# One-hot products of the gates in two passes of the rounded 32-bit type

## The chip, the cores and the metric

One core of a Trainium2 chip runs the program. The time is device microseconds of one execution. The kernel before took 3685.89 us, the median of 3 runs (3681.72 to 3691.2).

## The reference

Two transformer blocks run one after the other on 512 tokens of width 1024. The change lies in the expert layer (`peer`) of the first block. It has 16384 experts, 128 x 128 keys, and 8 heads that each choose 16 experts for a token:

```python
expert = k1 * PEER_N_KEYS + k2
g = jax.nn.softmax(top_s.astype(jnp.float32), axis=-1).astype(hb.dtype)
ue = expert_u[expert]
act = jax.nn.gelu(jnp.einsum('td,thkd->thk', hb, ue), approximate=False) * g
ve = expert_v[expert]
return jnp.einsum('thk,thkd->td', act, ve)
```

`k1` and `k2` are the two key numbers (0 to 127) of each of a token's 128 choices, and `g` is the choice's gate.

## The kernel before

**Two ways through the experts.** For 384 of the 512 tokens (token tiles 0, 1 and 2, called DENSE) the kernel computes the scores of all 16384 experts: 128 blocks b of 128 experts, each 24 products of 128 weights by 384 columns (`linear(("U", b), ...)`). The last 128 tokens (tile 3, SPARSE) take only their chosen rows, gathered by indirect DMAs from GpSimd (L718) and multiplied and summed on VectorE (L1957).

**Rounded type.** Products of weights use a rounded 32-bit type (fp32r): ScalarE copies a weight tile WR to its rounded high part WH (L1200), VectorE subtracts to get the low part WL (L1601), and TensorE makes three rounded products (high by high, high by low, low by high), all on L787. Other products, the one-hot ones among them, use the plain 32-bit type, which the profile records as two passes.

**The gates of the dense tokens.** The dense scores have to be multiplied by a gate for every (expert, token) pair, zero where the expert was not chosen. For one token this is a 128 x 128 matrix: the sum over its 128 choices of onehot(k2) times gate times onehot(k1). The kernel makes it as one product with the choices on the 128 partitions. The keys and gates of a token tile are first transposed (`keys_out`, three transposes on L992, after VectorE has finished the gates in `gates`, L1941), and VectorE copies them to KT (`keys_in`, L1975). Then, for four tokens at a time, 96 times in all:

- VectorE makes hotA, 1.0 where the column number equals k1 (`hots`, L1984, one instruction for four tokens).
- ScalarE multiplies hotA in place by the gate (`hot_weights`, L1375, four instructions).
- GpSimd makes hotB, 1.0 where the column number equals k2 (L734, four instructions with one operation each).
- TensorE multiplies them (`hot_gates`, L983, four products of 128 x 128 by 128 columns).
- ScalarE copies the bank out to Gs (`gates_out`), and SP's queue stores it to memory every fourth time.

**Order.** All of this is written out block by block in the loops over b on each engine. In block b, TensorE does the scores, then the transposes if b is GATE_AT + 1, then the one-hot products of group b - HOT_LAG (HOT_LAG is 2), then in some blocks a tile of the modulation (L865 and a small product on L787). GpSimd does in block b the four L734 of group b and then the gathers that are due, in one queue. VectorE does in block b the hotA of group b, the low half of the next weights, some steps of the choice of the next token tile (`choose`) and the row dot L1957. hotA and hotB have four buffers each (HOTS). TensorE waits for hot_a (counted by ScalarE) and hot_b (counted by GpSimd) before a group. The groups run in the blocks 22 to 53, 54 to 85 and 86 to 117 (HOT_AT).

Of the kernel before, what the change touches and what calls it, by code (L numbers as in the profile page):

```python
# [6 lines left out]
P = 128  # L7
# [416 lines left out]
def build(nc, plan, d, out):  # L424
# [9 lines left out]
    with ctx:  # L434
# [91 lines left out]
        def col(t, tt):  # L526
            return t[:, tt * P:(tt + 1) * P]
# [24 lines left out]
        Q2 = place("Q2", F0 + 8192, 2, T)  # L552
        Rw = place("Rw", F0 + 8192, 16, P)
        cand = place("cand", F0 + 10240, PH, NC)
        hotA, hotB = place("hotA", F0 + 12288, HOTS, 4, P), place("hotB", F0 + 14336, HOTS, 4, P)
        f1 = F0 + 16384
        top, topi, topf = (place(n_, f1 + 256 * i_, 16, PK)[:, :, :] for i_, n_ in enumerate(("top", "topi", "topf")))
        cv, ca, cb, kk1, kk2, gg, cpos, cpa = (
# [2 lines left out]
        top_of = {tt: (tab[:, 2048:2304], tab[:, 2304:2560]) for tt in EARLY[1:]}  # L561
        top_of = {tt: tuple(t_.rearrange("p (i k) -> p i k", k=PK) for t_ in pair) for tt, pair in top_of.items()}
        Re = {tt: place(f"Re{tt}", F0 + at, 8, P) for tt, at in zip(EARLY, (9216, 10240))}
        gsum, KT = place("gsum", f1 + 1792, 1, 16), place("KT", f1 + 1824, 2, 3, P)
        hT = place("hT", F0 + 18976, D)
        geU = place("geU", F0 + 20000, 2, TN)
        sub = tab[:, 0:2048].rearrange("p (s n) -> p s n", s=16)
# [137 lines left out]
        @block.gpsimd  # L705
        def _(pool):
            k = Counts(pool, plan)

            pool.wait_ge(sgu_loaded, 64)
            nc.gpsimd.affine_select(out=ws, in_=ws, pattern=[[0, 4], [1, P]], compare_op=ALU.is_ge,  # L710
                                           fill=0.0, base=0, channel_multiplier=-1).then_inc(ws_ready, k.inc(ws_ready))

            def gather(i):

                if i >= ROWS:
                    pool.wait_ge(row_used, i - ROWS + 1)
                table, pick = ("urows", i) if i < PICKS else ("vrows", i - PICKS)
                nc.gpsimd.indirect_dma_start(  # L718
                    rows[:, i % ROWS, :], None, d[table][:, :],
                    bass.IndirectOffsetOnAxis(ap=expert[:, pick:pick + 1].bitcast(u32), axis=0),  # L720
                ).then_inc(row_loaded[i % ROWS], 16)

            issued = 0
            for b in range(NK):
                if hot_in(b):
                    tt, q = hot_in(b)
                    n = tt * (P // 4) + q
                    if q == 0:
                        pool.wait_ge(dve_read, k.reading(dve_read, ("kt", tt)))
                    if n >= HOTS:  # L730
                        pool.wait_ge(filled, k.filling(filled, ("g", (n - HOTS) // 32, (n - HOTS) % 32)))
                    for t in range(4):
                        c = 4 * q + t
                        nc.gpsimd.tensor_scalar(hotB[:, n % HOTS, t, :], consts["iota128"][:, :],  # L734
                                                KT[:, tt % 2, 1, c:c + 1], None, ALU.is_equal)\
                            .then_inc(hot_b, k.inc(hot_b))
                if b >= GATE_AT[SPARSE]:
                    if issued == 0:
                        pool.wait_ge(xt_stored, 16)
                        pool.wait_ge(picked, 1)  # L740
                    while issued < dots_by(b) + ROWS:
                        gather(issued)
                        issued += 1
            while issued < 2 * PICKS:
                gather(issued)
                issued += 1
# [3 lines left out]
        def _(pe):  # L750
# [225 lines left out]
            def hot_gates(tt, q):  # L976
                n = tt * (P // 4) + q
                pe.wait_ge(hot_a, 4 * (n + 1))
                pe.wait_ge(hot_b, 4 * (n + 1))

                def calls(b):
                    for t in range(4):
                        yield nc.tensor.matmul(col(b, t), hotB[:, n % HOTS, t, :], hotA[:, n % HOTS, t, :],  # L983
                                               start=True, stop=True)
                fill(("g", tt, q), calls)

            def keys_out(tt):
                pe.wait_ge(kt_ready, k.next(kt_ready))

                def calls(b):  # L990
                    for n, src in enumerate((kk1, kk2, gg)):
                        yield nc.tensor.transpose(col(b, n), src.rearrange("p a b -> p (a b)"), consts["ident"][:, :])  # L992
                fill(("kt", tt), calls)

            for b in range(NK):
# [184 lines left out]
        def _(act):  # L1180
# [188 lines left out]
            def hot_weights(tt, q):  # L1369
                n = tt * (P // 4) + q  # L1370
                act.wait_ge(hot_keys, n + 1)
                for t in range(4):
                    c = 4 * q + t
                    hot = hotA[:, n % HOTS, t, :]
                    act.activation(hot, hot, ACT.Copy, scale=KT[:, tt % 2, 2, c:c + 1]).then_inc(hot_a, k.inc(hot_a))  # L1375

            def gates_out(tt, q):
                n = tt * (P // 4) + q
# [212 lines left out]
        def _(dve):  # L1591
# [342 lines left out]
            def gates(done):  # L1934
# [6 lines left out]
                v.tensor_tensor(gg, gg, gsum[:, 0, 8:16].unsqueeze(2).to_broadcast([P, PH, PK]), ALU.mult)\  # L1941
                    .then_inc(done, k.inc(done))

            def picks():

                dve.wait_ge(*k.own())
# [23 lines left out]
            def keys_in(tt):  # L1970
                if tt == 2:

                    dve.wait_ge(filled, k.filling(filled, ("g", 0, 31)))
                b = bank_of(("kt", tt))
                v.tensor_copy(KT[:, tt % 2, :, :].rearrange("p a b -> p (a b)"), b[:, 0:3 * P])\  # L1975
                    .then_inc(dve_read, k.inc(dve_read))

            def hots(tt, q):
# [10 lines left out]
            for b in range(NK):  # L1989
# [14 lines left out]
                for tt in DENSE:  # L2004
                    if b == GATE_AT[tt]:
                        for _ in following:
                            pass
                        gates(kt_ready)
                        following, steps = choose(tt + 1) if tt + 1 < SPARSE else iter(()), STEP
                for _ in range(steps):  # L2010
                    next(following, None)
# [438 lines left out]
```

## Time and profile before

| | |
|---|---|
| median of the runs | 3685.89 us |
| profiled execution, own time | 3694.17 us |
| its span in the trace | 3692.3 us |
| TensorE matmul busy | 3524.6 us (95%) |
| TensorE weight load busy | 3031.6 us (82%) |
| VectorE busy | 2061.6 us (56%) |
| ScalarE busy | 1487.7 us (40%) |
| GpSimd busy | 730.6 us (20%) |
| mean granted TensorE clock | 0.974 |

The shares are averages over the whole span; the one-hot products lie between 847 and 1377 us. PE is TensorE's matmuls and PEld its weight loads, DVE is VectorE, ACT ScalarE, POOL GpSimd. Matmuls overlap, so a record's duration is longer than the time from one record's start to the next.

### The profile page before, as it was taken

Reading aid. Unit: us, or ns where it says so; the run is one execution under the profiler, and the core shown is the slowest. Engines: PE = TensorE matmul, PEld = TensorE weight load, DVE = VectorE, ACT = ScalarE, POOL = GpSimd, SP = SyncE. Lnnn points to the kernel's source line nnn. Section 1 sums busy time; section 2 is a strip of 40 time slices with the busy share of each in tenths; the row PEclk is TensorE's granted clock in tenths of the full one; section 3 lists DMA queues with packets and bytes.
Section 4 is the critical chain, followed back from the end, with each engine's and each line's share of the span. In section 5 each row is a group of like instructions: output and inputs, shape, how many; then the busy total and the mean of one; then the engine's idle time right before and its main releaser. Section 6 shows DMA issues by size and latency. Waiting matters only on the chain.

```text
span 3692.3 us, 54725 instructions
## 1 busy us (share of the span) xinstructions
PE 3524.6 (95%) x21345; PEld 3031.6 (82%) x21345; DVE 2061.6 (56%) x4243; ACT 1487.7 (40%) x2664; POOL 730.6 (20%) x645
## 2 busy tenths in 40 slices
PE   7999999989999999999998999999999979999997
PEld 5787887879899999999996568868888756777886
DVE  3253344677887557888884563284333246547443
ACT  3233324336666663333334462263112345436222
POOL 0000000008999884443330000000000000000000
PEclk8999999999999999999998999999999979999998
DMA  6224323469888999999993011101121211221232
GB/s 227 97 81 148 103 97 123 158 217 303 272 294 284 324 310 358 376 360 365 373 364 111 29 35 58 63 7 58 58 66 62 91 57 46 75 69 36 95 99 91
DMA packets 219679, 594.50 MB, mean 161 GB/s; under 512 B 17824, under 2 KB 101408, under 8 KB 216096
## 3 DMA queue, kind: packets, MB, share of 16 engines
q1 hardware_dynamic: 159312, 405.84, 31.8%
q0 software_dynamic: 36864, 134.23, 10.2%
q10 hardware_dynamic: 23248, 50.92, 3.7%
q8 instruction: 172, 2.82, 0.3%
q14 instruction: 83, 0.68, 0.1%
HBM read 530.11 MB, written 60.82 MB: 160 GB/s over the span
## 4 chain that ended last, share of the span: by engine, by line
PE 88%; DVE 5%; ACT 3%; DMA 2%; issue 2%; ACTq 0%; POOL 0%; DVEq 0%; SPq 0%
PE bank L787 64%; PE bank L1016 14%; PE bank L1108 3%; PE bank L983 2%; PE bank L1094 2%; PE bank L811 1%; PE bank L865 1%; DMA WR<-in_weights 1%; DMA rows<-in_urows,rk 1%; PE bank L898 0%; DVE WL L1601 0%; PE bank L970 0%; DVE OF L2297 0%; DVE SrowA L2151 0%; DVE X L2300 0%
## 5 line engine op out<-in xcount | busy, mean ns | idle before, releaser
L1601 DVE TENSOR_TENSOR WL<-WR,WH 128x1024 fp32r<-128x1024 f32 x512 | 631.4, 1235 | 838.5 <-ACT WH L1200 787.5
L1200 ACT ACTIVATE WH<-WR 128x1024 fp32r<-128x1024 f32 x512 | 536.7, 1057 | 739.3 <-PE bank L1016 303.7
L787 PE MATMUL bank<-H2h,WH 128*128 128x512 f32 (+1 forms) x1624 | 580.4, 357 | 4.5 <-DVE H2l L1629 4.5
L787 PE MATMUL bank<-H2h,WL 128*128 128x512 f32 (+1 forms) x1624 | 575.7, 354 | 0.0
L787 PE MATMUL bank<-H2l,WH 128*128 128x512 f32 (+1 forms) x1624 | 575.3, 354 | 0.0
L787 PE MATMUL bank<-Hh,WH 128*128 128x384 f32 (+1 forms) x1440 | 522.1, 363 | 13.8 <-DVE WL L1601 13.8
L787 PE MATMUL bank<-Hh,WL 128*128 128x384 f32 (+1 forms) x1440 | 508.3, 353 | 0.0
L787 PE MATMUL bank<-Hl,WH 128*128 128x384 f32 (+1 forms) x1440 | 507.8, 353 | 0.0
L734 POOL TENSOR_SCALAR hotB<-iota,KT 128x128 f32<-128x128 f32 x384 | 396.9, 1045 | 3.2
L1016 PE MATMUL bank<-ah,WH 128*128 128x384 f32 x1024 | 345.3, 337 | 6.5 <-issue 3.6
L787 PEld LDWEIGHTS bank<-H2h,WH 128*128 128x128 f32 x1624 | 309.1, 190 | 49.9 <-issue 7.7
L787 PEld LDWEIGHTS bank<-H2h,WL 128*128 128x128 f32 x1624 | 309.2, 190 | 43.7 <-issue 1.9
L1016 PE MATMUL bank<-ah,WL 128*128 128x384 f32 x1024 | 344.7, 337 | 0.0
L1016 PE MATMUL bank<-al,WH 128*128 128x384 f32 x1024 | 344.7, 337 | 0.0
L787 PEld LDWEIGHTS bank<-H2l,WH 128*128 128x128 f32 x1624 | 308.5, 190 | 42.7
L718 POOL DMA_INDIRECT rows<-in_urows,rk x128 | 149.0, 1164 | 856.7 <-DVE rk L1951 698.7
L787 PEld LDWEIGHTS bank<-Hh,WH 128*128 128x128 f32 x1440 | 274.0, 190 | 31.7 <-DVE WL L1601 14.3
L787 PEld LDWEIGHTS bank<-Hl,WH 128*128 128x128 f32 x1440 | 272.9, 189 | 16.6
L787 PEld LDWEIGHTS bank<-Hh,WL 128*128 128x128 f32 x1440 | 273.8, 190 | 14.8
L718 POOL DMA_INDIRECT rows<-in_vrows,rk x128 | 183.8, 1436 | 283.5 <-DVE acc L1968 260.7
L1016 PEld LDWEIGHTS bank<-ah,WH 128*128 128x128 f32 x1024 | 194.1, 190 | 7.7 <-issue 4.5
L1016 PEld LDWEIGHTS bank<-ah,WL 128*128 128x128 f32 x1024 | 194.2, 190 | 0.0
(349 smaller groups left out, 5562.0 us busy)
## 6 DMA issues: line engine op xcount, KB each, us to landing
WR<-in_weights SPq DMA_DIRECT2D x498, 512.0 KB, 3.8
WR<-in_vrows SPq DMA_DIRECT2D x128, 512.0 KB, 6.6
gelu_by_expert<-geU ACTq DMA_DIRECT2D x128, 192.0 KB, 5.1
gates_by_expert<-tab SPq DMA_DIRECT2D x24, 1024.0 KB, 9.5
geV<-gelu_by_expert SPq DMA_DIRECT2D x32, 768.0 KB, 9.2
Gt<-gates_by_expert SPq DMA_DIRECT2D x14, 1536.0 KB, 12.8
x_kept<-X ACTq DMA_DIRECT2D x2, 3072.0 KB, 8.6
X<-x_kept ACTq DMA_DIRECT2D x2, 3072.0 KB, 10.4
```

The costliest lines, as they stand in the source:

```text
L718: nc.gpsimd.indirect_dma_start(rows[:, i % ROWS, :], None, d[table][:, :], bass.IndirectOffsetOnAxis(ap=expert[:, pick:pick + 1].bitcast(u ...
L734: nc.gpsimd.tensor_scalar(hotB[:, n % HOTS, t, :], consts["iota128"][:, :], KT[:, tt % 2, 1, c:c + 1], None, ALU.is_equal)\
L787: yield nc.tensor.matmul(b[0:rows, out_cols], a, r, start=n == 0, stop=n == len(pairs) - 1)
L811: last = nc.tensor.matmul(b, a, r, start=j == 0 and n == 0, stop=j == KD - 1 and n == 2)
L865: yield nc.tensor.matmul(b[p0:p0 + QUAD, 0:P], cs[:, j, :], w[:, j, :], start=j < QUADS, stop=j >= KD - QUADS)
L983: yield nc.tensor.matmul(col(b, t), hotB[:, n % HOTS, t, :], hotA[:, n % HOTS, t, :], start=True, stop=True)
L1016: mm = nc.tensor.matmul(bank[sums[dd].bank][:, 0:TN], a, r, start=c == 0 and n == 0, stop=c == NK - 1 and n == 2)
L1094: yield nc.tensor.transpose(col(b, t - t0), col(Srow[kind][u % 4], t), consts["ident"][:, :])
L1108: yield nc.tensor.matmul(b[p0:p0 + VB, 0:P], v_[:, t, 0:VB], PT[kind][:, u % 2, n_, :], start=n_ < 2, stop=n_ >= len(tiles) - 2)
L1200: act.activation(WH[:, n % SLOTS, :, :].rearrange("p a b -> p (a b)"), WR[:, c % SLOTS, :, :].rearrange("p a b -> p (a b)"), ACT.Copy)\
L1601: v.tensor_tensor(WL[:, n % SLOTS, :, :].rearrange("p a b -> p (a b)"), WR[:, plan.splits[n] % SLOTS, :, :].rearrange("p a b -> p (a b)"), ...
```

## The change

The gate is split on VectorE into a high part, `ghi` (the gate rounded to fp32r), and `grest`, the remainder divided by the high part. Both are transposed (four transposes instead of three). GpSimd's hotB becomes onehot(k2) times the high part, by a second operation with a second per-partition scalar. hotA stays a plain one-hot and is kept; ScalarE writes hotA times the ratio into a new buffer, hotR. TensorE makes two products per token into the same bank, hotB by hotA and hotB by hotR, all in fp32r. KT moves to another place and gets a fourth column block.

```diff
--- before.py
+++ after.py
@@ -552,7 +552,8 @@
         Q2 = place("Q2", F0 + 8192, 2, T)
         Rw = place("Rw", F0 + 8192, 16, P)
         cand = place("cand", F0 + 10240, PH, NC)
-        hotA, hotB = place("hotA", F0 + 12288, HOTS, 4, P), place("hotB", F0 + 14336, HOTS, 4, P)
+        hotA, hotB, hotR = (place(n_, F0 + at, HOTS, 4, P, dt=f32r)
+                            for n_, at in (("hotA", 12288), ("hotB", 14336), ("hotR", 6144)))
         f1 = F0 + 16384
         top, topi, topf = (place(n_, f1 + 256 * i_, 16, PK)[:, :, :] for i_, n_ in enumerate(("top", "topi", "topf")))
         cv, ca, cb, kk1, kk2, gg, cpos, cpa = (
@@ -561,7 +562,8 @@
         top_of = {tt: (tab[:, 2048:2304], tab[:, 2304:2560]) for tt in EARLY[1:]}
         top_of = {tt: tuple(t_.rearrange("p (i k) -> p i k", k=PK) for t_ in pair) for tt, pair in top_of.items()}
         Re = {tt: place(f"Re{tt}", F0 + at, 8, P) for tt, at in zip(EARLY, (9216, 10240))}
-        gsum, KT = place("gsum", f1 + 1792, 1, 16), place("KT", f1 + 1824, 2, 3, P)
+        gsum, KT = place("gsum", f1 + 1792, 1, 16), place("KT", F0 + 11264, 2, 4, P)
+        ghi, grest, grec = place("ghi", f1 + 1824, P, dt=f32r), place("grest", f1 + 1952, P), place("grec", f1 + 2080, P)
         hT = place("hT", F0 + 18976, D)
         geU = place("geU", F0 + 20000, 2, TN)
         sub = tab[:, 0:2048].rearrange("p (s n) -> p s n", s=16)
@@ -732,7 +734,8 @@
                     for t in range(4):
                         c = 4 * q + t
                         nc.gpsimd.tensor_scalar(hotB[:, n % HOTS, t, :], consts["iota128"][:, :],
-                                                KT[:, tt % 2, 1, c:c + 1], None, ALU.is_equal)\
+                                                KT[:, tt % 2, 1, c:c + 1], KT[:, tt % 2, 2, c:c + 1],
+                                                ALU.is_equal, ALU.mult)\
                             .then_inc(hot_b, k.inc(hot_b))
                 if b >= GATE_AT[SPARSE]:
                     if issued == 0:
@@ -981,15 +984,18 @@
                 def calls(b):
                     for t in range(4):
                         yield nc.tensor.matmul(col(b, t), hotB[:, n % HOTS, t, :], hotA[:, n % HOTS, t, :],
-                                               start=True, stop=True)
+                                               start=True, stop=False)
+                        yield nc.tensor.matmul(col(b, t), hotB[:, n % HOTS, t, :], hotR[:, n % HOTS, t, :],
+                                               start=False, stop=True)
                 fill(("g", tt, q), calls)
 
             def keys_out(tt):
                 pe.wait_ge(kt_ready, k.next(kt_ready))
 
                 def calls(b):
-                    for n, src in enumerate((kk1, kk2, gg)):
-                        yield nc.tensor.transpose(col(b, n), src.rearrange("p a b -> p (a b)"), consts["ident"][:, :])
+                    keys = [kk.rearrange("p a b -> p (a b)") for kk in (kk1, kk2)]
+                    for n, src in enumerate((*keys, ghi[:, :].bitcast(f32), grest[:, :])):
+                        yield nc.tensor.transpose(col(b, n), src, consts["ident"][:, :])
                 fill(("kt", tt), calls)
 
             for b in range(NK):
@@ -1371,8 +1377,8 @@
                 act.wait_ge(hot_keys, n + 1)
                 for t in range(4):
                     c = 4 * q + t
-                    hot = hotA[:, n % HOTS, t, :]
-                    act.activation(hot, hot, ACT.Copy, scale=KT[:, tt % 2, 2, c:c + 1]).then_inc(hot_a, k.inc(hot_a))
+                    act.activation(hotR[:, n % HOTS, t, :], hotA[:, n % HOTS, t, :].bitcast(f32), ACT.Copy,
+                                   scale=KT[:, tt % 2, 3, c:c + 1]).then_inc(hot_a, k.inc(hot_a))
 
             def gates_out(tt, q):
                 n = tt * (P // 4) + q
@@ -1941,6 +1947,21 @@
                 v.tensor_tensor(gg, gg, gsum[:, 0, 8:16].unsqueeze(2).to_broadcast([P, PH, PK]), ALU.mult)\
                     .then_inc(done, k.inc(done))
 
+            def gate_parts():
+
+                flat = gg.rearrange("p h j -> p (h j)")
+                dve.wait_ge(*k.own())
+                v.tensor_copy(ghi[:, :], flat).then_inc(dve_step, k.inc(dve_step))
+                dve.wait_ge(*k.own())
+                v.tensor_scalar(grec[:, :], ghi[:, :].bitcast(f32), 1e-30, None, ALU.max)\
+                    .then_inc(dve_step, k.inc(dve_step))
+                v.tensor_tensor(grest[:, :], flat, ghi[:, :].bitcast(f32), ALU.subtract)\
+                    .then_inc(dve_step, k.inc(dve_step))
+                dve.wait_ge(*k.own())
+                v.reciprocal(grec[:, :], grec[:, :]).then_inc(dve_step, k.inc(dve_step))
+                dve.wait_ge(*k.own())
+                v.tensor_tensor(grest[:, :], grest[:, :], grec[:, :], ALU.mult).then_inc(kt_ready, k.inc(kt_ready))
+
             def picks():
 
                 dve.wait_ge(*k.own())
@@ -1972,7 +1993,7 @@
 
                     dve.wait_ge(filled, k.filling(filled, ("g", 0, 31)))
                 b = bank_of(("kt", tt))
-                v.tensor_copy(KT[:, tt % 2, :, :].rearrange("p a b -> p (a b)"), b[:, 0:3 * P])\
+                v.tensor_copy(KT[:, tt % 2, :, :].rearrange("p a b -> p (a b)"), b[:, :])\
                     .then_inc(dve_read, k.inc(dve_read))
 
             def hots(tt, q):
@@ -2005,7 +2026,8 @@
                     if b == GATE_AT[tt]:
                         for _ in following:
                             pass
-                        gates(kt_ready)
+                        gates(dve_step)
+                        gate_parts()
                         following, steps = choose(tt + 1) if tt + 1 < SPARSE else iter(()), STEP
                 for _ in range(steps):
                     next(following, None)
```

## Rows read from the trace of the kernel before

**Rows 1.** Busy time by stretch: start:end us, length, then busy us and count per engine.
```profile
900.00:1000.00 100.00, 92.74 (x626) 88.88 (x626) 82.05 (x179) 60.40 (x123) 96.77 (x84) 0.98 0.79 265
1000.00:1100.00 100.00, 100.00 (x683) 98.69 (x682) 78.15 (x218) 68.42 (x139) 96.61 (x97) 1.00 0.93 313
```

**Rows 2.** Chain of waits from 865 to 900 us: start us, us, what.
```profile
870.39 0.89 PE bank L983 x8
871.28 4.16 PE bank L787 x24
...
881.38 0.57 PE bank L865 x16
881.96 4.58 PE bank L787 x26
```

**Rows 3.** Groups by line from 846 to 1378 us, busy us, mean ns, idle before.
```profile
L734 POOL TENSOR_SCALAR hotB<-iota,KT 128x128 f32<-128x128 f32 x377 | 392.0, 1051 | 3.2
...
L983 PE MATMUL bank<-hotA,hotB 128*128 128x128 f32 x768 | 103.7, 279 | 14.1 <-ACT hotA L1375 7.8 <-issue 6.3
```

**Rows 4.** GpSimd's line L734 alone: duration ns min/median/max, first and last start.
```profile
L734 POOL TENSOR_SCALAR hotB<-iota,KT x384: 590/627/3452, 838.1 to 1371.6; 128x128 f32<-128x128 f32 x192
```

**Rows 5.** GpSimd in order of time, 892 to 903 us: start us, us, what.
```profile
892.23 4.61 POOL L734 TENSOR_SCALAR hotB<-iota,KT 128x128 f32<-128x128 f32 x4
897.01 1.03 POOL L718 DMA_INDIRECT rows<-in_urows,rk  x1 [0.17 <-issue]
898.07 4.54 POOL L734 TENSOR_SCALAR hotB<-iota,KT 128x128 f32<-128x128 f32 x4
```

**Rows 6.** TensorE in order of time, same stretch, its one-hot products.
```profile
896.94 1.13 PE L983 MATMUL bank<-hotA,hotB 128*128 128x128 f32 x8 [0.29 <-issue]
...
902.71 1.13 PE L983 MATMUL bank<-hotA,hotB 128*128 128x128 f32 x8 [0.46 <-issue]
```

**Rows 7.** GpSimd in order of time, 1040 to 1050 us.
```profile
1040.04 3.85 POOL L734 TENSOR_SCALAR hotB<-iota,KT 128x128 f32<-128x128 f32 x4
1044.05 1.03 POOL L718 DMA_INDIRECT rows<-in_urows,rk  x1 [0.16 <-issue]
1045.11 4.31 POOL L734 TENSOR_SCALAR hotB<-iota,KT 128x128 f32<-128x128 f32 x4
```

**Rows 8.** VectorE in order of time, 1041.5 to 1043.6 us.
```profile
1041.63 1.26 DVE L1957 SCALAR_TENSOR_TENSOR rows<-rows,hT 128x1024 f32<-128x1024 f32 x1
...
1042.82 0.68 DVE L1984 TENSOR_TENSOR hotA<-iota,KT 128x512 f32<-128x512 f32 x1
```

**Rows 9.** TensorE in order of time: first and last of 19 rounded products, 256 columns.
```profile
189.75 0.28 PE L787 MATMUL bank<-WH,Hl 128*128 128x256 f32 x1
...
191.91 0.28 PE L787 MATMUL bank<-WH,Hl 128*128 128x256 f32 x1
```

**Rows 10.** TensorE's weight loads in order of time, from 848.5 us.
```profile
848.58 0.30 PEld L787 LDWEIGHTS bank<-fold,mrow 128*128 128x128 f32 x2 [0.20 <-issue]
848.80 0.19 PEld L787 LDWEIGHTS bank<-Hh,WH 128*128 128x128 f32 x1
```

**Rows 11.** Weight loads of the whole span by line and shape.
```profile
L787 PEld LDWEIGHTS bank<-Hh,WH 128*128 128x128 f32 x1440 | 274.0, 190 | 31.7 <-DVE WL L1601 14.3 <-issue 2.3
...
L983 PEld LDWEIGHTS bank<-hotA,hotB 128*128 128x128 f32 x768 | 99.4, 194 | 17.6 <-ACT hotA L1375 9.0 <-issue 8.6
L1108 PEld LDWEIGHTS bank<-PTB,vB 128*64 128x64 f32 x832 | 43.8, 136 | 13.8 <-issue 13.1 <-ACT PTB L1226 0.6
```

**Rows 12.** GpSimd's groups by line, the smallest.
```profile
L2441 POOL MEMSET const-float32-1.0<- 128x1 f32 x1 | 0.1, 99 | 0.0
```

**Rows 13.** VectorE's groups by line and shape.
```profile
L1647 DVE RECIPROCAL rt<-rt 128x128 f32<-128x128 f32 x5 | 4.7, 942 | 25.8 <-ACT rt L1226 25.8
...
L1736 DVE TENSOR_SCALAR SV<-SV,mv,rs 128x1024 f32<-128x1024 f32 x4 | 3.0, 812 | 0.1
...
L1965 DVE TENSOR_SCALAR acc<-rows,rk 128x1024 f32<-128x1024 f32 x2 | 1.5, 746 | 0.0
...
L1947 DVE COPY rk<-gg 128x128 f32<-128x128 f32 x1 | 0.2, 228 | 0.0
```

**Rows 14.** In order of time: VectorE's last step of the gates, TensorE's first transposes.
```profile
825.75 0.29 DVE L1941 TENSOR_TENSOR gg<-gg,gsum 128x128 f32<-128x128 f32 x1
...
831.22 0.38 PE L992 MATMUL bank<-ident,kk 128*128 128x128 f32 x2
```

## The prediction

> **What bounds the kernel now.** I read the busy time by stretch first. In [rows 1] the stretch from 900 to 1300 us is the one with the one-hot products, and two engines are full there at once. TensorE is busy 92.7 of 100 us in the first window and 100.0 of 100 in the second, and GpSimd 96.8 and 96.6. VectorE is at 82 and 78, ScalarE at 60 and 68. The chain of waits gives TensorE's rhythm [rows 2]: a block is 4.16 us of expert scores (24 products of 384 columns, 0.173 us each) and 0.89 us of one-hot products (4 products recorded as 8 passes, 0.111 us a pass). Every fourth block adds 0.57 us (L865) and some 0.42 us (two passes on L787) of modulation. So a block is 5.05 us, or 6.05 us with modulation, 5.30 us on average, and there are 96 with one-hot products.
>
> Grouping the stretch by line [rows 3] shows the change's share: L983 is 768 passes, which at 0.111 us of pitch are 85 us of TensorE; L734 on GpSimd is 377 instructions with a mean of 1051 ns, though the line's own view [rows 4] gives a shortest of 590 and a median of 627. Something stretches them, so I looked at GpSimd in order of time. At 892 to 903 us [rows 5] four L734 take 4.61 and 4.54 us, with 1.03 us of a gather between them, and start 5.84 us apart. The first group ends at 892.23 + 4.61 = 896.84, the next at 902.61. TensorE's one-hot products start at 896.94 and 902.71, each 0.10 us later, after 0.29 and 0.46 us idle [rows 6]. The profile calls that idle "issue", but the two ends fit a wait for hotB. So GpSimd already sets the pace in places. Where it does not, it is close behind: at 1040 us a group takes 3.85 us and the next starts 5.07 us after it [rows 7], TensorE's own 5.05. Why the instruction stretches is in VectorE's order of time: its two-input operations on the row dot (1.26 us) and on hotA (0.68 us) run from 1041.63 to 1043.50 [rows 8], and GpSimd's group ends at 1043.89, just after them.
>
> **TensorE's part.** Four products of the 32-bit type (8 passes) become eight of the rounded type, one pass each. The trace has no rounded product under 256 columns, so I bound one. Low end: 256 columns start 0.120 us apart ((191.91 - 189.75)/18, [rows 9]) and 384 columns 0.173 [rows 2]; on that line 128 columns are 0.067 us, a group 0.53 us, 0.36 us less than 0.89. High end: each is carried as dearly as a 32-bit product (2 x 0.111 = 0.223), a group 1.78 us, 0.89 more. Middle: the weight load sets the pitch. Two loads of 128 weights before products of only 3 columns start at 848.58 and the next product's load at 848.80, 0.11 us each with nothing else to wait for [rows 10]. Load durations are 136 ns for 64 weights and 190 ns for 128 [rows 11], 0.84 ns a weight, so 128 of them stream for about 0.11 us. The rounded product's load (on WH) lasts 190 ns, like the 32-bit one's 194. With 384 columns that load hides behind 0.173 us of columns; with 128 it cannot. So I take 0.111 to 0.120 us each, a group of 0.89 to 0.96 us: 0 to +0.07 us, over 96 groups 0 to +7 us.
>
> The Trainium skill states the load as columns over 1.2 GHz, which is 107 ns for 128 (TensorE: Matmul & The Clock Gate, LDWEIGHTS); the loads in [rows 10] agree with it. The Trainium skill's same page gives about 81 ns for load and product at 128 columns (Back-to-back issue gap). By that a group would be an estimated 0.65 us and TensorE would shed 23 us; no row here shows such a pitch.
>
> **GpSimd's part.** Each of the 384 L734 gets a second operation (a product) with a second per-partition scalar, and a rounded output. Low end: no dearer, 0 (the first operation and its columns stay, so a gain is excluded). High end: the shortest L734 lasts 590 ns [rows 4], and an instruction with almost nothing to do (a memset of one column) 99 ns [rows 12]; if the second operation costs all that the first does beyond that, it adds 0.49 us. The nearest rows are VectorE's: over 1024 columns one operation with one scalar is 746 ns, two with two scalars 812 ns [rows 13], 66 ns more. GpSimd is the slower engine per column (0.49 us over 128 columns, against 0.75 us over VectorE's 1024), so I lean upward from that row and take twice its difference, 0.12 us.
>
> A group grows by 4 x 0.12 = 0.48 us. What covers it? In [rows 7] nothing but the 0.16 us gaps: GpSimd is already busy 96.6 of 100 us, and its cycle is as long as TensorE's. When GpSimd falls behind, TensorE waits for hotB, and ScalarE's and VectorE's work of the next block starts from TensorE's; so VectorE's interference repeats once a block and does not shrink. Hence +0.48 us on each of 96 blocks, 46 us, and TensorE's 0 to 7 us disappear inside that wait. The lead that GpSimd has at the start (a few us) is spent once; I subtract 4.
>
> **VectorE's and ScalarE's part.** The hotA comparison and the scaling on L1375 keep their sizes; the scaling writes hotR where it wrote hotA, and ScalarE has 32 to 40 us of every 100 free [rows 1]. Three times, VectorE gets five small operations. Four at about the 0.23 us of the 128-column copy (L1947), and a reciprocal of 128 columns, 0.94 us [rows 13]: 1.9 us with gaps. The transposes wait for them: the gates were ready at 825.75 + 0.29 = 826.04 and the transposes started at 831.22 [rows 14], so 5.2 us of cover remain 3.3 us. Behind them on VectorE is the low half of the next weights (L1601), one block ahead of its use; at the third place VectorE is near full, so I count 2 us of the 3 x 1.9. The fourth transpose costs 3 x 0.11 and the wider copy as little: 0.5 us.
>
> **The sum.** 46 - 4 + 2 + 0.5 = 44, rounded up to 47 for the clock that falls a little where TensorE waits more (0.98 in the window at 900 with 7.3 us idle, [rows 1]). The profiled execution took 3694.2 us (span 3692.3 and 1.9 around it), 8.3 above the median of the runs, 3685.9. So 3741 for that one, 3733 as a median.
>
> **The rivals.**
> (1) The rounded product of 128 columns is as dear as a 32-bit one. For: no row shows one under 256 columns. Against: the line from 384 to 256 columns shows no bend. A block grows 0.89 us, GpSimd's added 0.48 hides behind it, and the waits for hotB that exist today (up to the 14.1 us idle before L983, [rows 3]) go: 96 x 0.89 = 85, less 10, 3761.
> (2) The other side: the weight load does not set the pitch and the second operation is free on GpSimd. Then TensorE's block is 4.69 us and GpSimd's cycle decides how much is kept. GpSimd ran at 5.07 us between starts in [rows 7] and 5.84 in [rows 5], and the DMA engines are busy 0.93 of the window at 1000 us [rows 1]; of 0.36 x 96 = 34 us I let 20 through: 3666. It decides only if the addition on GpSimd is under about 0.05 us an instruction. The Trainium skill speaks for this half: a GpSimd body of at most two operations is bound by its port, not by its operations (GPSIMD Engine Reference, Elementwise). No row here has two operations there.
> (3) Both are neutral: the pitch is 0.111 and GpSimd's addition is under 0.03 us. 3690.
> (4) GpSimd's second operation is near its upper bound (0.3 us or more): 96 x 1.2 = 115, 3800.
>
> **How the numbers follow.** The forecast has 0.42, rival (1) 0.22, (2) 0.13, (3) 0.14, (4) 0.09. What a measurement can tell from no change is 0.3%, 11 us. Faster: 0.12, from (2). Slower: the forecast, (1) and (4), 0.73, less its small tail, 0.71. The rest, 0.17, is within. The range runs from 3672 to 3795: it leaves out the deeper half of (2) and most of (4).
>
> **What would show it.** L983's pitch: eight records in 0.89 us to 0.96 (forecast), 0.53 (rival 2), 1.78 (rival 1). L734's shortest duration: about 0.1 us longer. TensorE idle before L983 in most blocks, ending 0.10 us after a GpSimd group, and VectorE emptier by share. Wrong would be a TensorE that is full through the stretch with blocks of 5.05 us, or L734 unchanged.

## The result, and the profile after

The changed kernel took 3757.12 us (median of 4 runs, 3755.31 to 3759.35), the kernel before on the same chip 3683.80 us (4 runs, 3681.35 to 3691.20). The ratio is 1.0196, with an interval of 1.0181 to 1.0210: 72 us slower, where the forecast had added 47. The forecast was 3733, and the measured time lies inside the range of 3672 to 3795. The profiled execution after took 3755.31 us, its span 3753.4 and the mean granted clock 0.971.

The stage with the one-hot products holds the difference. Before, its first and last product (L983) started at 847.0 and 1376.1 us, 529.1 us apart; after, those of L986 and L988 at 846.6 and 1442.2, 595.6 us apart, 66.5 more. The first fence is the busy time by stretch of the kernel before, for that stage and for a later window than [rows 1] shows; the second is the kernel after, with the stage and the windows that answer to [rows 1]. Columns: start:end, length, then busy us and count of TensorE, its weight loads, VectorE, ScalarE and GpSimd, then the granted clock, the DMA share and GB/s.

```profile
846.90:1376.10 529.20, 513.61 (x3490) 502.32 (x3489) 385.77 (x824) 342.83 (x697) 493.98 (x467) 0.99 0.89 298
1200.00:1300.00 100.00, 97.08 (x652) 95.49 (x651) 55.79 (x75) 62.72 (x131) 88.42 (x86) 0.98 0.94 327
```

```profile
846.60:1442.20 595.60, 541.79 (x3489) 522.78 (x3490) 388.78 (x834) 346.70 (x698) 574.25 (x468) 0.95 0.79 264
900.00:1000.00 100.00, 88.12 (x569) 84.27 (x568) 72.34 (x180) 55.32 (x114) 96.90 (x79) 0.96 0.79 261
1000.00:1100.00 100.00, 92.57 (x594) 89.52 (x594) 73.02 (x177) 59.86 (x119) 95.59 (x80) 0.94 0.75 248
1200.00:1300.00 100.00, 89.35 (x588) 86.18 (x587) 59.99 (x79) 58.60 (x116) 96.86 (x81) 0.97 0.81 288
```

Read the stage rows as two balances. On GpSimd, busy time grew by 80.3 us (493.98 to 574.25) with the same instructions, and its idle time fell from 35.2 to 21.4, by 13.9: together the 66.4 us. On TensorE, with the same number of matmuls, idle time grew from 15.6 to 53.8 us and busy time from 513.61 to 541.79; the clock granted went from 0.99 to 0.95, so the same work took longer between the waits. In the windows shown GpSimd is now full (95.6 to 96.9 of 100 us) and TensorE is not (88 to 93), where [rows 1] had TensorE at 100.0 in one of them.

The profiled execution of the kernel before was 8 to 10 us above the medians of that kernel, and its stage was long. In run e4 (below), where all engines do the same work and only GpSimd's output type differs, the stage is this:

```profile
846.40:1365.10 518.70, 508.82 (x3489) 499.45 (x3489) 384.29 (x815) 342.60 (x697) 490.76 (x469) 1.00 0.90 304
```

Against it the stage after is 76.9 us longer, with 83.5 more of GpSimd's busy time and 6.6 less of its idle time. The 66.5 and the 76.9 us stand on either side of the 72 of the medians.

Next, the line of the hotB comparison alone, after (duration ns min/median/max, first and last start), answering to [rows 4], and the groups by line from 846 to 1450 us, answering to [rows 3] (busy us, mean ns, idle before).

```profile
L736 POOL TENSOR_SCALAR hotB<-iota,KT x384: 780/806/3458, 837.2 to 1438.9; 128x128 fp32r<-128x128 f32 x192
```

```profile
L736 POOL TENSOR_SCALAR hotB<-iota,KT 128x128 fp32r<-128x128 f32 x378 | 453.0, 1206 | 3.7
...
L720 POOL DMA_INDIRECT rows<-in_urows,rk x92 | 124.0, 1348 | 21.6 <-issue 14.6 <-DVE rows L1978 7.0
...
L986 PE MATMUL bank<-hotA,hotB 128*128 128x128 f32 x384 | 92.2, 277 | 54.2 <-issue 30.9 <-ACT hotR L1380 23.3
```

The shortest hotB comparison went from 590 to 780 ns, 0.190 us longer, the median from 627 to 806. The mean went from 1051 to 1206, 0.155 more: 384 x 0.155 = 60 us. The gathers on the same engine stood so before, in the groups by line from 846 to 1376 us:

```profile
L718 POOL DMA_INDIRECT rows<-in_urows,rk x90 | 103.1, 1146 | 30.6 <-DVE rows L1957 16.5 <-issue 14.1
```

They went from 1146 to 1348 ns, 0.202 more: 92 x 0.202 = 19 us. 60 + 19 = 79 of the 80.3 us. And what they waited for VectorE's row dot fell from 16.5 us to 7.0. TensorE's idle time before the one-hot products went from 14.1 to 54.2 us. Its list of waits in the same stretch says how often (who <- for whom: us, times, longest):

```profile
PE bank L986 <- issue: 30.9, 23, 4.2
PE bank L986 <- ACT hotR L1380: 23.3, 17, 2.6
```

These are 40 waits, in 96 blocks.

The rhythm behind it is in GpSimd's order of time, after, answering to [rows 5]; beneath it TensorE's first product of each block.

```profile
1057.31 5.39 POOL L736 TENSOR_SCALAR hotB<-iota,KT 128x128 fp32r<-128x128 f32 x4
1062.87 1.82 POOL L720 DMA_INDIRECT rows<-in_urows,rk  x1 [0.17 <-issue]
...
1071.06 4.21 POOL L736 TENSOR_SCALAR hotB<-iota,KT 128x128 fp32r<-128x128 f32 x4
1075.44 1.74 POOL L720 DMA_INDIRECT rows<-in_urows,rk  x1 [0.17 <-issue]
1077.22 4.05 POOL L736 TENSOR_SCALAR hotB<-iota,KT 128x128 fp32r<-128x128 f32 x4
```

```profile
1062.80 0.30 PE L986 MATMUL bank<-hotA,hotB 128*128 128x128 f32 x1 [1.22 <-ACT hotR L1380]
...
1075.37 0.30 PE L986 MATMUL bank<-hotA,hotB 128*128 128x128 f32 x1 [1.06 <-ACT hotR L1380]
...
1081.37 0.30 PE L986 MATMUL bank<-hotA,hotB 128*128 128x128 f32 x1 [0.70 <-issue]
```

The groups of four end at 1057.31 + 5.39 = 1062.70, 1071.06 + 4.21 = 1075.27 and 1077.22 + 4.05 = 1081.27. TensorE starts 0.10 us after each, after 1.22, 1.06 and 0.70 us idle. The releaser named is ScalarE's hotR twice and "issue" once; the ends fit GpSimd's group all three times.

Where GpSimd is ahead, TensorE's own block is what it was. This is the chain of waits after, around 1050 us, answering to [rows 2] (start us, us, what).

```profile
1047.22 4.22 PE bank L790 x24
1051.44 0.06 PE bank L986
1051.50 0.11 PE bank L988
...
1052.29 4.22 PE bank L790 x24
```

Eight rounded products start 0.11 us apart, and the block is 1052.29 - 1047.22 = 5.07 us where it was 5.05.

### The profile page after: what moved, and what is told of

Its sections match the earlier page's. It is cut to its first block, busy times and chain, and to the rows that moved or that the text cites. A ratio compares the mean times of both kernels' runs of the same rounds, so it can differ in the third digit from the quotient of the medians.

```text
span 3753.4 us, 54746 instructions
## 1 busy us (share of the span) xinstructions
PE 3547.4 (95%) x21348; PEld 3045.0 (81%) x21348; DVE 2065.4 (55%) x4258; ACT 1491.6 (40%) x2664; POOL 810.5 (22%) x645
## 4 chain that ended last, share of the span: by engine, by line
PE 87%; DVE 5%; ACT 3%; DMA 3%; issue 2%; POOL 0%; ACTq 0%; SPq 0%; DVEq 0%
PE bank L790 63%; PE bank L1022 13%; PE bank L1114 2%; PE bank L1100 2%; DMA WR<-in_weights 1%; PE bank L868 1%; PE bank L986 1%; PE bank L814 1%; PE bank L988 1%; DMA rows<-in_urows,rk 1%; DVE WL L1607 1%; ACT hotR L1380 1%; PE bank L901 0%; DVE SrowA L2173 0%; PE bank L973 0%
## 5 line engine op out<-in xcount | busy, mean ns | idle before, releaser
L790 PE MATMUL bank<-Hh,WL 128*128 128x384 f32 (+1 forms) x1440 | 516.3, 359 | 0.0
L790 PE MATMUL bank<-Hl,WH 128*128 128x384 f32 (+1 forms) x1440 | 515.8, 358 | 0.0
L736 POOL TENSOR_SCALAR hotB<-iota,KT 128x128 fp32r<-128x128 f32 x384 | 458.4, 1201 | 3.8
L720 POOL DMA_INDIRECT rows<-in_urows,rk x128 | 169.7, 1326 | 840.2 <-DVE rk L1972 697.0
```

The source lines that it names most:

```text
L720: nc.gpsimd.indirect_dma_start(rows[:, i % ROWS, :], None, d[table][:, :], bass.IndirectOffsetOnAxis(ap=expert[:, pick:pick + 1].bitcast(u ...
L790: yield nc.tensor.matmul(b[0:rows, out_cols], a, r, start=n == 0, stop=n == len(pairs) - 1)
```

## The experiments

Each ratio is to the kernel before on the same chip; "after with" and "before with" say which kernel was edited. e9b_wide_one_op and e10_half_weights are one run each, so their times carry no interval.

**One operation in hotB** (after with).
```diff
-    KT[:, tt % 2, 1, c:c + 1], KT[:, tt % 2, 2, c:c + 1], ALU.is_equal, ALU.mult)
+    KT[:, tt % 2, 1, c:c + 1], None, ALU.is_equal)
```


> The changed kernel with one thing undone: hotB is made by one operation again (the comparison alone, written in the rounded type); its factor, the gate's high part, is left out, so the gates are wrong and the work is otherwise the same. Theory G (GpSimd's second operation is the loss): the shortest hotB instruction falls from 780 ns to about 590, the idle time before TensorE's one-hot products from 54 us to about 14, and the time to 3680 to 3692 us (before 3684). Theory T (the eight rounded products, or the extra VectorE steps, are the loss): GpSimd is quicker but the time stays above 3735 us.

Measured: 3684.84 us, ratio 0.9989 (0.9978 to 1.0001). All of the loss is gone, with the eight rounded products, the gates' five steps and the fourth transpose still there. The first line is that of hotB alone in this kernel, the second is from its groups by line, 846 to 1378 us.
```profile
L736 POOL TENSOR_SCALAR hotB<-iota,KT x384: 590/627/3455, 840.2 to 1362.4; 128x128 fp32r<-128x128 f32 x192
```
```profile
L985 PE MATMUL bank<-hotA,hotB 128*128 128x128 f32 x384 | 86.2, 264 | 4.7 <-issue 3.5 <-ACT hotR L1379 1.1
```
The instruction is back at 590 ns, and TensorE waits 4.7 us before the products instead of 54.2.

**The second operation alone, in the kernel before**, with a second per-partition scalar (a column of ones), and then with a constant. The third puts only the rounded output type into the kernel before.
```diff
-    KT[:, tt % 2, 1, c:c + 1], None, ALU.is_equal)
+    KT[:, tt % 2, 1, c:c + 1], ones[:, 0:1], ALU.is_equal, ALU.mult)   # e2; e3 has 1.0 for ones[:, 0:1]
```


> The kernel before with one part of the change alone: the second operation on GpSimd, a product with a per-partition scalar (a column of ones, so the values stay). Theory G: shortest instruction 780 ns, time 3745 to 3765 us. Theory T: no more than 3700 us.

> As the run before it, but the second scalar is the constant 1.0 in the instruction. It splits the 190 ns: if fetching a second per-partition scalar costs it, the shortest instruction is near 590 to 640 ns and the time 3684 to 3705 us; if the second operation over 128 columns costs it, 780 ns and 3745 to 3765 us. I expect the larger part from the operation: 700 to 780 ns, about 3735 us.

```diff
-    hotB = place("hotB", F0 + 14336, HOTS, 4, P)
+    hotB = place("hotB", F0 + 14336, HOTS, 4, P, dt=f32r)
-    nc.tensor.matmul(col(b, t), hotB[:, n % HOTS, t, :], ...)
+    nc.tensor.matmul(col(b, t), hotB[:, n % HOTS, t, :].bitcast(f32), ...)
```


> The kernel before with hotB written in the rounded type by one operation and read as plain 32-bit by TensorE, so only GpSimd's output type changes. If rounding is part of the 190 ns, the shortest instruction is above 620 ns and the time above 3695 us; if not (what I expect), 590 ns and 3684 us, within 0.3%.

Measured: e2 3751.63 us, ratio 1.0174 (1.0155 to 1.0194); e3 3715.50, 1.0073 (1.0055 to 1.0092); e4 3685.71, 0.9996 (0.9985 to 1.0007). The line of hotB alone in the three kernels:
```profile
L734 POOL TENSOR_SCALAR hotB<-iota,KT,ones x384: 780/804/3422, 834.4 to 1430.9; 128x128 f32<-128x128 f32 x192
```
```profile
L734 POOL TENSOR_SCALAR hotB<-iota,KT x384: 704/730/3457, 837.0 to 1393.0; 128x128 f32<-128x128 f32 x192
```
```profile
L734 POOL TENSOR_SCALAR hotB<-iota,KT x384: 590/627/3451, 839.2 to 1360.6; 128x128 fp32r<-128x128 f32 x192
```
So the 0.190 us are 704 - 590 = 114 ns for the operation and 780 - 704 = 76 ns for taking its scalar from a tile; the rounding costs nothing. The one edit of e2, with every other part of the change absent, gives 65 of the 72 us, and the intervals of e2 and of the change overlap. The second operation with its second scalar is therefore the cause: it alone brings the loss (e2), and its removal alone takes it away (e1). The duration in e3 came as expected (700 to 780 ns), its time is a miss: I expected about 3735, and it came 20 us lower. Its windows (columns as above) show why:
```profile
1000.00:1100.00 100.00, 94.08 (x636) 89.81 (x635) 71.69 (x201) 63.94 (x127) 96.78 (x86) 0.98 0.79 265
1200.00:1300.00 100.00, 98.75 (x674) 97.13 (x673) 57.81 (x81) 66.00 (x136) 91.59 (x90) 1.00 0.96 340
```
In the first, GpSimd is full and TensorE is not; in the second, TensorE is at 98.75 and GpSimd at 91.59. In the later part of the stage GpSimd has spare time, 88.42 busy of 100 in the kernel before and 93.50 in the same window of e4, and much of an addition of 0.46 us a group still fits there. I had read [rows 1] as the whole stage.

**Half of the products** (after with).
```diff
-    yield matmul(col(b, t), hotB[...], hotA[...], start=True, stop=False)
-    yield matmul(col(b, t), hotB[...], hotR[...], start=False, stop=True)
+    yield matmul(col(b, t), hotB[...], hotA[...], start=True, stop=True)
```


> The changed kernel with the second product of each token left out (the low part of the gate is missing), so TensorE has 4 rounded products in a group and not 8: about 0.45 us less in each of 96 blocks, 43 us if TensorE set the pace. Theory G (GpSimd sets it): the freed time turns into waiting for hotB, at most 10 us are gained, the time is 3745 to 3757 us. Theory T: 3714 us.

Measured: 3768.37 us, ratio 1.0228 (1.0200 to 1.0255), a miss by time: I expected at most 3757, no slower than the changed kernel (1.0196). The two intervals overlap. From its groups by line, 846 to 1378 us, and its busy time by stretch:
```profile
L986 PE MATMUL bank<-hotA,hotB 128*128 128x128 f32 x336 | 54.7, 288 | 76.5 <-issue 44.4 <-ACT hotR L1378 31.8
```
```profile
1000.00:1100.00 100.00, 83.58 (x486) 80.23 (x487) 71.56 (x162) 54.91 (x108) 97.09 (x76) 0.88 0.71 229
```
TensorE was relieved of four products a block and only waited more: 76.5 us by 1378 us of the span, at a granted clock of 0.88 in that window. GpSimd stayed at 97. So TensorE's part of the change carries none of the loss. The 11 us between the two medians (on different chips) are not explained. In the profiled stages they sit in GpSimd's busy time (584.10 us in e5, 574.25 in the changed kernel), with the mean of hotB at 1249 ns against 1206; what stretches it more, no run separates.

**Two of the four hotB comparisons on VectorE** (after with, nothing left out).
```diff
-    for t in range(4):                       # GpSimd
+    for t in range(2):
-    pe.wait_ge(hot_b, 4 * (n + 1))
+    pe.wait_ge(hot_b, 2 * (n + 1))
+    pe.wait_ge(hot_d, 2 * (n + 1))
...
+    for t in range(2, 4):                    # VectorE, behind hotA
+        c = 4 * q + t
+        v.tensor_scalar(hotB[:, n % HOTS, t, :], iota128, KT[:, tt % 2, 1, c:c + 1],
+                        KT[:, tt % 2, 2, c:c + 1], ALU.is_equal, ALU.mult).then_inc(hot_d, k.inc(hot_d))
```


> The changed kernel, complete, with GpSimd's work halved: of the four hotB instructions of a group VectorE makes two (one instruction each with both operations, I estimate 0.25 us), GpSimd the other two. Theory G: GpSimd falls to about 70% busy, the idle time before the one-hot products nearly vanishes, and the time is at most that of the kernel before: 3672 to 3690 us. A rival: VectorE, at 72 to 78% in that stretch, cannot take 0.5 us more a block, and the weights' low halves come late: above 3700 us.

Measured: 3688.62 us, ratio 1.0011 (1.0001 to 1.0021). The whole change is kept, and 68 of 72 us are back. Its busy time by stretch, its VectorE hotB line, and TensorE's line:
```profile
1000.00:1100.00 100.00, 100.00 (x684) 98.88 (x683) 95.33 (x265) 66.20 (x138) 70.65 (x58) 1.00 0.91 301
```
```profile
L2012 DVE TENSOR_SCALAR hotB<-iota,KT x192: 331/390/953, 841.5 to 1358.9; 128x128 fp32r<-128x128 f32 x192
```
```profile
L988 PE MATMUL bank<-hotA,hotB 128*128 128x128 f32 x384 | 86.3, 264 | 2.0 <-ACT hotR L1382 2.0
```
TensorE is back at 100.00 of 100 and waits 2.0 us before the products. GpSimd has fallen to 70.65, and VectorE took its place as the fullest helper, 95.33. The rival that the weights' low halves come late is there in small: TensorE's list of waits, 846 to 1378 us, has this line:

```profile
PE bank L791 <- DVE WL L1609: 9.6, 2, 4.8
```

**The same in the kernel before** (edit as above, with `None, ALU.is_equal`).

> The kernel before, complete, with VectorE making two of the four hotB instructions of a group. Theory G says GpSimd was the co-limit already: the 14 us idle before the one-hot products go, 3672 to 3680 us. If those waits had another cause, or VectorE has no room: 3684 us or more.

Measured: 3684.35 us, ratio 0.9994 (0.9985 to 1.0003), a miss: I expected a gain. From its groups by line (846 to 1378 us), and from its list of waits in the same stretch (who <- for whom: us, times, longest):
```profile
L985 PE MATMUL bank<-hotA,hotB 128*128 128x128 f32 x768 | 101.3, 275 | 1.6 <-ACT hotA L1377 1.6
```
```profile
PE bank L788 <- DVE WL L1603: 7.6, 2, 3.8
```
The same two in e4, whose engines do the work of the kernel before, without the length of that one execution:
```profile
L983 PE MATMUL bank<-hotA,hotB 128*128 128x128 f32 x768 | 101.5, 275 | 6.9 <-issue 3.5 <-ACT hotA L1375 3.3
```
```profile
PE bank L787 <- DVE WL L1601: 3.0, 2, 1.5
```
So about half of the 14.1 us of waiting that I had expected back belonged to the profiled execution of the kernel before alone. From 6.9 to 1.6 us are 5.3 less, and the waits for the low half of a weight (WL) went from 3.0 to 7.6, 4.6 more: the busier VectorE hands it over late. The two cancel, as the times do. TensorE, full at 100.00 of 100 around 1000 us, has little left to win without less work of its own.

**What a single pass is worth** (before with one rounded product for each), alone and with the hotB split.
```diff
-    hotA, hotB = place("hotA", ...), place("hotB", ...)
+    hotA, hotB = place("hotA", ..., dt=f32r), place("hotB", ..., dt=f32r)
...
-    act.activation(hot, hot, ...)
+    act.activation(hot, hot.bitcast(f32), ...)
```


> The kernel before with its four products made rounded (one pass each, hotA with the gate rounded; the gate's low part is left out) and everything else as it was. TensorE has 0.45 us less in a block, 43 us over 96. If GpSimd was already the co-limit in the kernel before, as the prediction read it, most of that is lost to waits for hotB: a gain of 10 to 20 us, 3666 to 3676 us. If GpSimd had slack there: 3643 us.

> As the run before it (the gate's low part left out), and VectorE makes two of the four hotB instructions of a group. It takes away GpSimd's limit: 3640 to 3655 us if GpSimd was what held the run before back; the same as that run if it was not.

Measured: e11 3680.49 us, ratio 0.9987 (0.9974 to 1.0000), a miss: I expected a gain of 10 to 20 us. One of its ten runs took 13374.73 us, for a reason that nothing shows; the median of the other nine is 3678.79. e12 3650.37 us, ratio 0.9906 (0.9881 to 0.9931), as expected. TensorE's line, 846 to 1378 us, in e11 and in e12:
```profile
L983 PE MATMUL bank<-hotA,hotB 128*128 128x128 f32 x384 | 57.6, 273 | 35.1 <-ACT hotA L1375 19.7 <-issue 15.4
```
```profile
L985 PE MATMUL bank<-hotA,hotB 128*128 128x128 f32 x384 | 54.1, 263 | 3.7 <-ACT hotA L1377 3.6
```
Half of TensorE's one-hot passes gone is 96 x 4 x 0.111 = 43 us of its work. Alone that returns 5 to 7 us (3685.32 to 3680.49, or 3678.79) and turns into 35.1 us of waiting; relieving GpSimd alone returned 3 (e8, within noise); both together return 35 us. This shows that GpSimd was as much the bound as TensorE in the kernel before. e12 beats both kernels, by leaving out the gate's low part.

**What sets the pitch of a 128-column product** (after with one operation in hotB). The first makes one product over 256 columns (hotA and hotR together) in place of two, the second loads 64 weights in place of 128 with the columns unchanged.
```diff
-    yield matmul(col(b, t), hotB[...], hotA[...], start=True, stop=False)
-    yield matmul(col(b, t), hotB[...], hotR[...], start=False, stop=True)
+    yield matmul(b[:, (t % 2) * 256:(t % 2) * 256 + 256], hotB[...], hotAR[:, 0:4:3, at:at + P], start=True, stop=True)
```


> A measurement of TensorE's rounded product, in the changed kernel with hotB made by one operation: the two products of a token become one with 256 moving columns (hotR and hotA side by side), so one weight load of 128 serves both; tokens 2 and 3 overwrite the results of 0 and 1, and the sum of the two parts is left out. Theory L (the load of 128 weights sets the pitch of the 128-column product): four products start 0.120 us apart, 0.48 us a group where the changed kernel has 0.89. If instead a rounded product costs by its columns alone, the 256 columns take 0.21 us.

```diff
-    yield matmul(col(b, t), hotB[:, n % HOTS, t, :], hotA[...], ...)
+    yield matmul(col(b, t)[0:64], hotB[:, n % HOTS, t, 0:64], hotA[...], ...)   # hotR alike
```


> A measurement: the changed kernel with hotB made by one operation, and each of the eight products of a group with only 64 weights (the first half of hotB's columns; half of the result's rows are left out), 128 moving columns as before. Theory L: the pitch falls from 0.11 us to 0.06 to 0.07 us. Theory C (a rounded product of 128 columns runs at two cycles a column whatever the load): it stays at 0.11 us.

The chain of waits of the first kernel, then TensorE in order of time in the second:
```profile
1024.24 0.47 PE bank L986 x4
1024.71 4.17 PE bank L789 x24
```
```profile
1017.82 0.22 PE L985 MATMUL bank<-hotA,hotB 128*64 128x128 f32 x1
1017.88 0.22 PE L987 MATMUL bank<-hotR,hotB 128*64 128x128 f32 x1
...
1018.24 0.22 PE L987 MATMUL bank<-hotR,hotB 128*64 128x128 f32 x1
```
Twice the columns with one load: 0.47 / 4 = 0.12 us a product, hardly more than the 0.11 of 128 columns. Half the weights with the same columns: (1018.24 - 1017.82) / 7 = 0.060 us. The pitch halves with the weights and barely moves with the columns, so at 128 columns the weight load sets it. Both took about the time of the kernel before (3690.21 and 3680.03 us): TensorE's 40 us fewer bought nothing visible, much as in e11.

## Why the prediction was right, and where its sizes were off

**What bounds the kernel.** Right: GpSimd was full and as slow as TensorE. e11 and e12 show it directly, 5 to 7 us against 35 for the same relief of TensorE.

**TensorE's part, 0 to +7 us.** Right: the load sets the pitch (e10, e9b), the block went from 5.05 to 5.07 us, and with hotB back at one operation the kernel is at 0.9989 of before (e1). With [rows 10] the load's 0.11 us was there to be read before any 128-column rounded product existed. Rival (1) would have shown as a group of 1.78 us and falls; so does rival (2), which needed both a pitch of 0.067 and a free operation. One reason of the prediction was empty: two points, 256 and 384 columns, always lie on a line, so "no bend" said nothing about 128.

The Trainium skill gives 107 ns for the load of 128 weights (TensorE: Matmul & The Clock Gate, LDWEIGHTS), and the 0.11 us here agree. Its 81 ns for load and product at 128 columns (same page, Back-to-back issue gap) is not met by this type.

**GpSimd's part, +46 us.** The mechanism was right, the duration mis-sized: I took 0.12 us for the second operation, twice VectorE's 66 ns of [rows 13]; it measured 0.190 (780 against 590). By that the term is 4 x 0.190 x 96 = 73 us. The row that I doubled already held both prices, the operation and the second scalar from a tile (at 128 columns VectorE's two together are 61 ns, 270 against 331). What failed is the factor of two from VectorE to GpSimd, for which I had no row; it is about three (190 against 61). That the operation by a constant costs 0.114 us, close to my 0.12, is chance. Rival (4) had the right direction and too much of it; rival (3) needed under 0.03.

The Trainium skill's rule that a GpSimd body of at most two operations is bound by its port (GPSIMD Engine Reference, 3.1 Elementwise) is about the cost of each element, and would make the addition there nothing. e3 shows 114 ns for the operation alone at 128 columns, and the measurement decides for this instruction. Whether these 114 ns come with each element or once in each instruction is open, since no run varies the columns.

**"What covers it?"** My answer, nothing but the gaps of 0.16 us, failed in part. In the stage GpSimd gave up 13.9 us of idle time, 9.5 of them waits for the row dot before a gather (6.6 us against the stage of e4, so the size is known only roughly); in the window at 1200 us it had been busy only 88.42 of 100. I subtracted 4. e2 lost 65 us where 73 were added, e3 29 or so (3715.50 against 3686.19) where 44 were. Both errors, a price too low and a cover too small, pulled against each other. The step held in the part of the stage that [rows 1] shows, and I carried it to the rest.

**What I left out.** GpSimd's gathers became 0.202 us longer on average, 19 us in all; the hotB comparisons' stretch over their shortest shrank from 0.461 to 0.426 us (mean less minimum). That the interference "does not shrink" was thus nearly right for hotB and missed the gathers. e2 shows the same longer gathers without any other part of the change (mean 1382 ns up to 1376 us), so the new steps of VectorE do not make them. Nor does GpSimd's slower instruction: e11 has them too, with hotB at its 590 ns. Its lines from 846 to 1376 us:

```profile
L734 POOL TENSOR_SCALAR hotB<-iota,KT 128x128 fp32r<-128x128 f32 x380 | 370.0, 986 | 3.2
L718 POOL DMA_INDIRECT rows<-in_urows,rk x94 | 126.6, 1346 | 31.1 <-DVE rows L1957 16.5 <-issue 14.6
```

There the gathers took 23.5 us more than in the kernel before (103.1) and the comparisons 22.0 less (392.0), with a sum of 496.6 us against 495.1. What is common to e2, e11 and the changed kernel is a TensorE that waits for GpSimd; it looks as if the same interference falls on the gathers instead of the comparisons. So the 19 us of the gathers and the 13 by which the stretch of hotB shrank belong together, about 6 us net. The mechanism was not tried.

**VectorE's part, +2 us, and the fourth transpose, +0.5.** The five steps took 2.0 us, from 824.51 to 826.52, where I had 1.9. Here is VectorE after in order of time:
```profile
824.51 0.23 DVE L1954 CAST ghi<-gg 128x128 fp32r<-128x128 f32 x1
824.77 0.23 DVE L1956 TENSOR_SCALAR grec<-ghi 128x128 f32<-128x128 f32 x1
824.92 0.29 DVE L1958 TENSOR_TENSOR grest<-gg,ghi 128x128 f32<-128x128 f32 x1
825.24 0.95 DVE L1961 RECIPROCAL grec<-grec 128x128 f32<-128x128 f32 x1
826.23 0.29 DVE L1963 TENSOR_TENSOR grest<-grest,grec 128x128 f32<-128x128 f32 x1
```
The transposes started at 830.1 and waited for none of it: cover as forecast. Outside the stage the profiled spans leave 3163.2 us before and 3157.8 after, so nothing of these terms is to be seen there. Since e1 carries them all and is at 0.9989, they cost nothing that can be measured, where I had counted 2.5.

**The clock.** I rounded up 3 us for it. It fell more, from 0.99 to 0.95 over the stage, and TensorE's busy time grew by 28 us for the same matmuls. It was lowest in this window of the changed kernel:

```profile
1300.00:1400.00 100.00, 90.35 (x563) 87.50 (x562) 47.72 (x66) 55.81 (x114) 96.92 (x79) 0.91 0.78 259
```

GpSimd is as full there (96.92) as in the windows at a clock of 0.96 or 0.97. So I read TensorE's slower work as filling time in which it would have waited, and count nothing for it beside the 66 us of GpSimd's balance. No run holds the clock, so this is argued and not shown.

**The sum again.** 73 for the second operation, 19 for the gathers, -13 for the stretch that shrank (384 x 0.035), -14 of cover: 65 us, against 66.5 in the stage. With the time outside 5 us shorter, that is the 61 us between the two profiled executions; the one before was 8 to 10 us above the medians of that kernel, which makes it some 70. This is a balance of two executions and no second proof. Between e2 (1.0174) and the change (1.0196) some 5 to 8 us remain, and the intervals overlap. The stage of e2 is this:

```profile
844.40:1433.60 589.20, 531.59 (x3488) 510.42 (x3489) 383.85 (x824) 347.94 (x698) 568.65 (x466) 0.97 0.79 266
```

It is 6.4 us shorter than that of the change, and GpSimd is busy 5.6 us less in it (568.65 against 574.25). So what remains lies in GpSimd's stretched instructions as well; what in the change stretches them more is open.

**The signs.** The pitch came (eight products in 0.89 us), the shortest comparison grew by 0.190 us where I had said about 0.1, and VectorE became emptier (72.34 and 73.02 of 100 us, from 82.05 and 78.15). One sign failed: TensorE was to be idle before the products in most blocks, and it waited 40 times in 96 (11 times before). The added time is therefore not 0.48 us "on each of 96 blocks"; it comes in fewer and longer waits, 1.36 us on average, with blocks such as those at 1047 us between them.

## What to carry to other kernels

When a change trades work between engines, price the helper engine first: with two engines full, the time went with the slower cycle, and 43 us less of TensorE's work were worth 5 to 7 us until GpSimd was relieved and 35 us after. Read the busy share in every stretch of a stage and not only in its first windows, since cover sits where the other engine is emptier. If a second operation must be added to an instruction on a full engine, a scalar from a tile and a constant have different prices; and the same instruction can be shared out to another engine, which here returned 68 of 72 us and filled VectorE to 95 of 100.

## What the runs showed of the hardware that was not expected

- On GpSimd, a 128x128 comparison took 590 ns at least, 704 with a second operation by a constant, 780 with a second operation by a scalar from a tile; the rounded output added nothing (590). VectorE's figures for the first and the last are 270 (e12) and 331 ns (e7): its second operation with a scalar costs 61 ns at least, a third of GpSimd's 190. By the medians it is more, 281 against 390 ns.
- The rounded type at 128 columns and 128 weights started every 0.11 us, as fast as one of the two passes of the 32-bit type [rows 2]; at 64 weights every 0.060, and at 256 columns with 128 weights every 0.12.
- GpSimd's gathers lasted 1146 ns on average before, 1348 after, 1382 in e2 and 1346 in e11, with the same data to fetch. In e11 the comparisons became as much shorter, so that the two together took the same time (496.6 us against 495.1).
